# Modulation blocks of two row blocks by 512 columns instead of four by 256, and the sums of both layers as 48 rows of one full PSUM bank

## The chip, the cores and the metric

One core of a Trainium2 chip runs the whole program. The metric is the device time in microseconds of one execution; lower is better. TensorE does the matrix products, VectorE and ACT (ScalarE) the element-wise work, SyncE (SP) issues the weight loads, and ACT and GpSimd issue some small ones. TensorE writes to PSUM, eight banks of 512 fp32 columns a partition.

## The reference

Two blocks in a row, for 256 tokens of width 2048, fp32. The first mixes a gated linear recurrence, an mLSTM and a block attention, projects, adds, and attends to a memory. The second has two layers (a pooling layer, then latent attention with 16 heads), and each layer is steered by modulations, which are what the change is about:

```python
shift, scale, gate = jnp.split(jax.nn.silu(c) @ ada_w[i] + ada_b[i], 3, axis=-1)
h_lat = rms_norm_2(x, pre_norm[i]) * (1 + scale[:, None]) + shift[:, None]
shift_c, scale_c, gate_c = jnp.split(jax.nn.silu(c_ctx) @ ada_w[i] + ada_b[i], 3, axis=-1)
h_ctx = rms_norm_2(ctx, pre_norm[i]) * (1 + scale_c) + shift_c
...
x = x + gate[:, None] * rms_norm_2(y_lat, post_norm[i])
```

`ada_w` is 2 layers x 2048 rows x 6144 columns, 96 MB of the kernel's 307 MB read, and it is multiplied by two vectors only (c for the latents, c_ctx for the context). The columns of a layer are shift (2048), scale (2048) and gate (2048). They aren't needed before the second block: shift and scale of layer 0 before `pu3`, the gate of layer 0 before `po`, layer 1's shift and scale before `cq`, its gate before the last product's results are used.

## The kernel before, in words

**Weight products.** Each product (`Product`, a list in the order of the program: kv, win_a, win_b, win_c, mixo, xq, xo, the pool products pu, pg and pgate, po, then cq, mg01, ckv, kr, mg23, eight pairs of uq and ukv, mo) is cut into column groups of 512 and chunks of 512 rows. SP loads a chunk into `raw` (two slots). ACT rounds it into `w_high` (`act_high`, L289), VectorE puts the rest into `w_low` (`dve_low`, L299), and TensorE does three matmuls for each 128x128 block (L484 to L486, `pe_block`): high by high, high by low, low by high, 256 columns for one sequence or 512 for two, 48 in a full chunk. Results are taken out of PSUM by ACT or VectorE. Each engine follows the list in its own order, written out by hand; between engines there are semaphores only.

**Modulations.** They are computed beside the products. A *unit* is 512 KB of `ada_w`: four blocks of 128 rows by 256 columns, loaded by SP (`sp_unit`, L261, into `ada_raw`, two slots, waiting on `ada_link` until the unit two back is used up). VectorE (`dve_unit`) takes each block times a column of silu(c), one value a partition, and adds it to `ada_acc`, for both vectors: eight passes a unit, TENSOR_SCALAR (L410) for the first of a block's sums and SCALAR_TENSOR_TENSOR (L414) for the others. Each pass waits on `ada_link` for the one two back, which wrote the same half. After four units (2048 rows) `ada_acc` holds partial sums on 128 partitions for 256 columns, a *block* of modulations. TensorE sums over the partitions (`pe_ada`, L432, here called a *slab*): one fp32 matmul for each vector, whose weights are `PICK`, 48 columns of zeros with one column of ones at row r, so that the sums come into row r of a 48-row region of PSUM and nothing is added to the other rows. The next block's first pass on VectorE waits for the slab (`ada_summed`). There are 48 blocks, 24 a layer, and 192 units.

**Where the units stand.** `UNITS` gives each chunk its units: kv four in all, win_a, win_c, the pu chunks and xo one, mixo three in four chunks, pg, pgate and po two, each uq and ukv two, moba four. A chunk on VectorE is: `dve_low`, what the stage adds, then its units. Where a unit is a block's last, TensorE does the slab within that chunk (`pe_chunk`: after the second half's second tile), in moba after the last head, and in the attention pairs (`pe_pairs`) for pair a = 0 to 7 ahead of the product tile uq 1 and the scores.

**Rows.** The first 40 slabs go to bank 4, layer 0 in columns 0 to 255, layer 1 in 256 to 511; row 24 v + m for vector v and block m. Three times ACT copies the 48 rows (`act_rows`, L447, 256 columns) and TensorE turns them (`pe_rows`, L467, two transposes) so that VectorE can add the biases and gains (`dve_mods`, `dve_gates`): turn 0 after slab 16 (end of mixo), turn 1 after 24 (in pgate3: ACT's copy at its chunk 0, the transposes at chunk 1, VectorE at chunk 2), turn 2 after 40 (latents). Slabs 16 and 24 wait until the copy before is done. The last eight go to bank 3, which the ukv products use too; VectorE adds each to `LAST_ROWS` (`dve_last_rows`, L456, L458) and turn 3 takes that (mo).

**The attention pairs.** In each step j TensorE does uq and ukv of pair j and the attention of pair a = j - 1, interleaved. VectorE has per pair four units, the maxima (L2309), the reciprocal and scaling of the probabilities (L2315, L2316; TensorE transposes them in L2179), the output product (L2321), and ahead of the next scores (L2168, L2169) the rope (L2147 to L2150). The third unit stands before the scaling of the fourth quarter's probabilities, the fourth unit before that quarter's output product.

**Small things.** 24 vectors (gains, biases, c) come in as rows of `VROW`, 12 loads on ACT's queue and 12 on GpSimd's, are turned by four transposes (L714) and copied to `vectors` (512 columns). `ident`, `blockmask` and `mlmask` have tiles of their own and are loaded by ACT at the start; `mlmask` is first used in mgates (L1098), `blockmask` in mproj (L1160).

Of the kernel before, what the change touches and what calls it, by code (L numbers as in the profile page):

```python
# [8 lines left out]
ACT = mybir.ActivationFunctionType  # L9
# [3 lines left out]
P = 128  # L13
# [61 lines left out]
def vectors(a):  # L75
# [6 lines left out]
        ("lru_conv_w", m(a["lru_conv_w"][0]), 16), ("lru_conv_b", v(a["lru_conv_b"][0]), 4),  # L82
        ("lru_ba", v(a["lru_ba"][0]), 4), ("lru_bx", v(a["lru_bx"][0]), 4), ("lru_lambda", v(a["lru_lambda"][0]), 4),
        ("ml_conv_w", m(a["ml_conv_w"][0]), 24), ("ml_conv_b", v(a["ml_conv_b"][0]), 6),
        ("ml_g", v(a["ml_norm_g"][0]), 6), ("xa_g", v(a["xa_norm_g"][0]), 16), ("final_g", v(a["final_norm_g"]), 16),
        ("ada_b0", v(a["ada_b_2"][0]), 48), ("ada_b1", v(a["ada_b_2"][1]), 48),
        ("pre0", v(a["pre_norm_2"][0]), 16), ("pre1", v(a["pre_norm_2"][1]), 16),
        ("post0", v(a["post_norm_2"][0]), 16), ("post1", v(a["post_norm_2"][1]), 16),
        ("pool_b", v(a["pool_b_grp_2"].rearrange("l g c -> l (g c)")[0]), 16),
        ("pool_s", v(a["pool_scale_2"][0]), 16),  # L90
        ("q_g", v(a["mla_q_norm_2"][0]), 4), ("kv_g", v(a["mla_kv_norm_2"][0]), 4),
# [32 lines left out]
def build(nc, a, out):  # L124
# [52 lines left out]
    with ctx:  # L177
# [30 lines left out]
        assert at <= 4 * P  # L208
        VROW = BIG[:, 76:78, :].rearrange("p a t -> p (a t)")
# [3 lines left out]
        blockmask = sb("blockmask", [P, P])  # L213
        mlmask = sb("mlmask", [P, P])
# [17 lines left out]
        consts_in, vec_in = [sem(f"consts_in{n}") for n in range(3)], [sem("vec_in_act"), sem("vec_in_pool")]  # L232
# [168 lines left out]
        def dve_unit(dve, u):  # L401
            part, us = u % 4, u % 2
            dve.wait_ge(ada_loaded[us], 16 * (u // 2 + 1))
            if part == 0 and u >= 4:

                dve.wait_ge(ada_summed, u // 4)
            for k in range(KC):
                for v in range(2):
                    if part == 0 and k == 0:
                        ins = nc.vector.tensor_scalar(ACC[:, v], ARAW[:, us, k], SC[:, v, 0:1], None, ALU.mult)  # L410
                    else:

                        dve.wait_ge(ada_link, 8 * u + 2 * k + v - 1)
# [2170 lines left out]
```

## Time and profile before

| | |
|---|---|
| Three runs | 2092.23 us median (2091.14 to 2093.05) |
| The profiled execution, its own time | 2092.57 us |
| its span | 2090.8 us |
| TensorE busy | 1846.7 us, 88% |
| VectorE busy | 1534.3 us, 73%; of it L414 583.6, L410 29.7 |
| ACT busy | 809.6 us, 39% |
| TensorE's mean granted clock | 0.922 of full |
| read from HBM | 307 MB, 148 GB/s |
| slabs (L432, L435) | 43.2 + 8.5 us of TensorE, 192 records for 96 matmuls |

The span goes from the first to the last instruction; 1.8 us lie around it. Busy times of one engine are unions, so overlapping instructions count once, and a mean duration can be longer than the distance from one start to the next. An fp32 matmul shows as two records. L12 is line 12 of the kernel. In the rows below a bracket gives the engine's idle time before the instruction and what ended it, and "x4" is a run of four instructions merged into one row, from the first start to the last end.

### The profile page before, as it was taken

What the parts mean: (1) busy time and instruction counts of PE and PEld (TensorE: products, weight loads), DVE (VectorE), ACT (ScalarE), POOL (GpSimd) and SP (SyncE); (2) the same over time, 40 slices, a digit from 0 to 9 for tenths busy, and PEclk for the clock granted to TensorE, in tenths of its full rate; (3) what the DMA queues carried; (4) which work ended last, traced back from release to release, by engine and by line L of the source; (5) the groups of instructions that cost most, each with busy time, mean ns of one, the idle gap of its engine ahead of it and who ended that gap; (6) DMA issues with size and microseconds to landing.
All of it is one profiled execution on the core that took longest, in us unless ns stands there. A gap on an engine that the chain in (4) does not pass through costs nothing.

```text
span 2090.8 us, 27915 instructions
## 1 busy us (share of the span) xinstructions
PE 1846.7 (88%) x10648; PEld 1567.9 (75%) x10648; DVE 1534.3 (73%) x3022; ACT 809.6 (39%) x1269; POOL 7.2 (0%) x18
## 2 busy tenths in 40 slices
PE   7999914599969987899999998999789989999797
PEld 6899903489939976687877886877687876666497
DVE  5888674598768866788779887977872577777444
ACT  6543334143334443423333222333553454443243
POOL 1000000000000000000000000000000000000000
PEclk9999956589969988899999999999899999999798
DMA  6688600068717633434536553654341553333252
GB/s 209 204 263 261 210 0 1 10 219 264 239 61 262 202 101 102 133 109 149 172 123 202 175 195 125 207 184 141 101 142 56 163 166 121 116 111 105 73 182 96
DMA packets 217954, 311.16 MB, mean 149 GB/s; under 512 B 14760, under 2 KB 121560, under 8 KB 217820
## 3 DMA queue, kind: packets, MB, share of 16 engines
q1 hardware_dynamic: 211328, 305.70, 44.9%
q10 hardware_dynamic: 6044, 3.56, 0.6%
q8 instruction: 84, 1.38, 0.3%
q14 instruction: 50, 0.41, 0.1%
q0 software_dynamic: 448, 0.12, 0.0%
HBM read 307.23 MB, written 2.10 MB: 148 GB/s over the span
## 4 chain that ended last, share of the span: by engine, by line
PE 46%; DVE 12%; ACT 3%; issue 1%; DMA 0%; DVEq 0%; ACTq 0%
PE bank L484 13%; PE bank L485 13%; PE bank L486 13%; DVE ada_acc L414 4%; DVE w_low L299 2%; PE bank L2169 2%; PE bank L2168 2%; PE bank L2188 1%; PE bank L432 1%; ACT w_high L289 1%; DVE big L643 1%; PE bank L2179 1%; DVE big L2011 0%; DVE big L2010 0%; PE bank L1650 0%
## 5 line engine op out<-in xcount | busy, mean ns | idle before, releaser
L484 PE MATMUL bank<-operand,w_high 128*128 128x256 f32 (+1 forms) x2720 | 872.6, 321 | 37.4 <-DVE operand L638 13.7
L485 PE MATMUL bank<-operand,w_high 128*128 128x256 f32 (+1 forms) x2720 | 861.1, 317 | 0.0
L486 PE MATMUL bank<-operand,w_low 128*128 128x256 f32 (+1 forms) x2720 | 860.3, 316 | 0.0
L484 PEld LDWEIGHTS bank<-operand,w_high 128*128 128x128 f32 x2720 | 525.3, 193 | 96.2 <-issue 31.1
L289 ACT ACTIVATE w_high<-raw 128x1024 fp32r<-128x1024 f32 (+4 forms) x416 | 397.0, 981 | 501.1 <-PE bank L486 304.5
L414 DVE SCALAR_TENSOR_TENSOR ada_acc<-ada_raw,silu_c,ada_acc 128x256 f32<-128x256 f32 x1440 | 583.6, 482 | 2.1 <-DMA ada_raw<-in_ada_w 0.6
L299 DVE TENSOR_TENSOR w_low<-raw,w_high 128x1024 fp32r<-128x1024 f32 (+4 forms) x416 | 454.0, 1130 | 176.6 <-ACT w_high L289 175.5
L486 PEld LDWEIGHTS bank<-operand,w_low 128*128 128x128 f32 x2720 | 525.1, 193 | 31.3
L485 PEld LDWEIGHTS bank<-operand,w_high 128*128 128x128 f32 x2720 | 525.6, 193 | 30.4
L484 PE MATMUL bank<-operand_small,w_high 128*128 128x512 f32 (+1 forms) x320 | 124.8, 390 | 11.6 <-DVE big L397 5.4
L485 PE MATMUL bank<-operand_small,w_high 128*128 128x512 f32 (+1 forms) x320 | 120.7, 377 | 0.0
L486 PE MATMUL bank<-operand_small,w_low 128*128 128x512 f32 (+1 forms) x320 | 120.5, 377 | 0.0
L484 PEld LDWEIGHTS bank<-operand_small,w_high 128*128 128x128 f32 x320 | 62.9, 197 | 28.9 <-DVE w_low L299 9.8
L486 PEld LDWEIGHTS bank<-operand_small,w_low 128*128 128x128 f32 x320 | 62.8, 196 | 10.8
L485 PEld LDWEIGHTS bank<-operand_small,w_high 128*128 128x128 f32 x320 | 63.1, 197 | 9.2
L410 DVE TENSOR_SCALAR ada_acc<-ada_raw,silu_c 128x256 f32<-128x256 f32 x96 | 29.7, 351 | 54.6 <-PE bank L432 53.4
L334 ACT ACTIVATE big<-bank 128x256 f32<-128x256 f32 x87 | 33.4, 384 | 93.3 <-PE bank L486 92.8
L2250 ACT ACTIVATE big<-bank,small 128x512 f32<-128x512 f32 x32 | 22.0, 689 | 102.6 <-DVE small L2310 99.3
L344 ACT ACTIVATE big<-bank 128x512 f32<-128x512 f32 x53 | 31.3, 598 | 65.2 <-PE bank L486 65.0
L2309 DVE TENSOR_REDUCE small<-bank 128x1 f32<-128x512 f32 x32 | 22.1, 691 | 44.2 <-PE bank L2169 44.2
L432 PE MATMUL bank<-ada_acc,row_picker 128*48 128x256 f32 x160 | 43.2, 393 | 4.0 <-DVE ada_acc L414 4.0
L628 ACT ACTIVATE operand<-big,modulations 128x256 fp32r<-128x256 f32 x64 | 30.8, 505 | 40.9 <-DVE big L643 40.8
(338 smaller groups left out, 1432.6 us busy)
## 6 DMA issues: line engine op xcount, KB each, us to landing
ada_raw<-in_ada_w SPq DMA_DIRECT2D x192, 512.0 KB, 4.0
raw<-in_w_in SPq DMA_DIRECT2D x96, 512.0 KB, 5.2
raw<-in_pool_w_in SPq DMA_DIRECT2D x64, 512.0 KB, 4.9
raw<-in_mla_w_in SPq DMA_DIRECT2D x48, 512.0 KB, 4.5
raw<-in_w_out SPq DMA_DIRECT2D x32, 512.0 KB, 5.5
raw<-in_pool_w_out SPq DMA_DIRECT2D x32, 512.0 KB, 6.0
raw<-in_mla_w_out SPq DMA_DIRECT2D x32, 512.0 KB, 4.6
raw<-in_xa_wkv SPq DMA_DIRECT2D x16, 512.0 KB, 4.7
```

The source lines that it names most:

```text
L289: ins = nc.scalar.activation(view(HI[:, slot, ks, :], False), view(RAW[:, slot, ks, :], True), ACT.Copy)
L299: ins = nc.vector.tensor_sub(view(LO[:, slot, ks, :], False), view(RAW[:, slot, ks, :], True), view(HI[:, slot, ks, :], False).bitcast(F32))
L334: nc.scalar.activation(dest_ap(p, i, n), PB[p.bank[i, n]][:, 0:T], ACT.Copy).then_inc(act_freed, 1)
L344: nc.scalar.activation(d, src, ACT.Copy).then_inc(act_freed, 1)
L414: ins = nc.vector.scalar_tensor_tensor(ACC[:, v], ARAW[:, us, k], SC[:, v, part * KC + k:part * KC + k + 1], ACC[:, v], ALU.mult, ALU.add)
L432: ins = pe.matmul(PB[4][0:48, 256 * layer:256 * layer + 256], PICK[:, 47 - r:95 - r], ACC[:, v, :], start=m == 0 and v == 0, stop=m in (23 ...
L484: pe.matmul(out_, hi, x[:, 0, :], start=first, stop=False, skip_group_check=True)
L485: pe.matmul(out_, hi, x[:, 1, :], start=False, stop=False, skip_group_check=True)
L486: return pe.matmul(out_, lo, x[:, 0, :], start=False, stop=last, skip_group_check=True)
L628: nc.scalar.activation(n["dst"](k, 0), hf_tile(n, k), ACT.Identity, bias=n["shift"](k)).then_inc(xh_ready, 1)
L2168: pe.matmul(bank[:, :], tile(q_of(a)[h])[:, qt * P:(qt + 1) * P], k_of(a, h), start=True, stop=False)
L2169: la_pe.inc(pe.matmul(bank[:, :], BIG[r, q_of(a)[2], qt * P:(qt + 1) * P], KRT[r, :], start=False, stop=True), "s", a, u)
```

## The change

A block becomes 512 columns wide and a unit two row blocks of 128 instead of four, so that a unit is still 512 KB and there are still 192 of them at the same places, but a block now takes eight units and there are 24 blocks. A unit is four passes of 512 columns. Slabs are half as many, with 512 columns each, at every second place of the old ones; all of them go to row 24 layer + 12 v + m of one region, the whole of bank 4 (the first 20) or bank 3 (the last four, after pairs 1, 3, 5 and 7). The rows are copied with 512 columns and turned by four transposes. Turn 0 comes after slab 8, at the same place; turn 1 after slab 13, and moves from pgate3 to pgate2 (ACT at chunk 2, TensorE at chunk 3) and pgate1 (VectorE at chunk 0); turn 2 after slab 20, at the same place; turn 3 as before. `ada_acc` grows by 512 columns, and to make room `vectors` shrinks to 384 columns (three transposes, the vectors in another order and so split otherwise over the two queues, 12 and 12), and the two masks get places in `big` that are free when they are loaded: `mlmask` in mgates and `blockmask` in mproj, ahead of their three weight loads, both on ACT's queue.

```diff
-        ARAW = sb("ada_raw", [P, 2, KC, 256])
-        ACC = sb("ada_acc", [P, 2, 256])
+        ARAW = sb("ada_raw", [P, 2, 2, GW])
+        ACC = sb("ada_acc", [P, 2, GW])
...
-        PV = sb("vectors", [P, 4 * P])
+        PV = sb("vectors", [P, 3 * P])
...
-        blockmask = sb("blockmask", [P, P])
-        mlmask = sb("mlmask", [P, P])
+        blockmask, mlmask = BIG[:, 46, P:2 * P], BIG[:, 18, 0:P]
...
         def sp_unit(sp, u):
-            part, us = u % 4, u % 2
+            part, us = u % 8, u % 2
             if u >= 2:
-                sp.wait_ge(ada_link, 8 * (u - 1))
-            b = u // 4
-            layer, col = b // 24, (b % 24) * 256
-            src = a["ada_w_2"][layer, part * KC * P:(part + 1) * KC * P, col:col + 256]
+                sp.wait_ge(ada_link, 4 * (u - 1))
+            layer, m = divmod(u // 8, 12)
+            src = a["ada_w_2"][layer, 2 * part * P:2 * (part + 1) * P, GW * m:GW * (m + 1)]
...
         def dve_unit(dve, u):
-            part, us = u % 4, u % 2
+            part, us = u % 8, u % 2
             dve.wait_ge(ada_loaded[us], 16 * (u // 2 + 1))
-            if part == 0 and u >= 4:
-
-                dve.wait_ge(ada_summed, u // 4)
-            for k in range(KC):
+            if part == 0 and u >= 8:
+
+                dve.wait_ge(ada_summed, u // 8)
+            for k in range(2):
                 for v in range(2):
                     if part == 0 and k == 0:
                         ins = nc.vector.tensor_scalar(ACC[:, v], ARAW[:, us, k], SC[:, v, 0:1], None, ALU.mult)
                     else:
 
-                        dve.wait_ge(ada_link, 8 * u + 2 * k + v - 1)
+                        dve.wait_ge(ada_link, 4 * u + 2 * k + v - 1)
                         ins = nc.vector.scalar_tensor_tensor(ACC[:, v], ARAW[:, us, k],
-                                                             SC[:, v, part * KC + k:part * KC + k + 1], ACC[:, v],
+                                                             SC[:, v, 2 * part + k:2 * part + k + 1], ACC[:, v],
                                                              ALU.mult, ALU.add)
...
-            if b in (16, 24):
-                pe.wait_ge(rows_moved, 1 if b == 16 else 2)
-            layer, m = divmod(b, 24)
+            if b in (8, 13):
+                pe.wait_ge(rows_moved, 1 if b == 8 else 2)
+            layer, m = divmod(b, 12)
             for v in range(2):
-                r = 24 * v + m
-                if b < 40:
-                    ins = pe.matmul(PB[4][0:48, 256 * layer:256 * layer + 256], PICK[:, 47 - r:95 - r], ACC[:, v, :],
-                                    start=m == 0 and v == 0, stop=m in (23, 15) and v == 1, skip_group_check=True)
+                r = 24 * layer + 12 * v + m
+                if b < 20:
+                    ins = pe.matmul(PB[4][0:48, :], PICK[:, 47 - r:95 - r], ACC[:, v, :], start=b == 0 and v == 0,
+                                    stop=b == 19 and v == 1, skip_group_check=True)
                 else:
-                    ins = pe.matmul(PB[3][0:48, 0:256], PICK[:, 47 - r:95 - r], ACC[:, v, :], start=v == 0, stop=v == 1)
+                    ins = pe.matmul(PB[3][0:48, :], PICK[:, 47 - r:95 - r], ACC[:, v, :], start=v == 0, stop=v == 1)
...
-            for n in range(2):
-                ins = pe.transpose(PB[TURN_BANK[turn]][:, 48 * n:48 * n + 48],
-                                   (ROWS[turn] if turn < 3 else LAST_ROWS)[:, n * P:(n + 1) * P], ident[0:48, 0:48])
+            for n in range(4):
+                ins = pe.transpose(PB[TURN_BANK[turn]][:, 48 * n:48 * n + 48], ROWS[turn][:, n * P:(n + 1) * P], ident[0:48, 0:48])
...
         def slab_after(p, i, j):
-            done = [u // 4 for u in UNITS[p.name, i, j] if u % 4 == 3]
+            done = [u // 8 for u in UNITS[p.name, i, j] if u % 8 == 7]
...
             act.dma_start(SEL, a["sel"]).then_inc(sel_in, 16)
+            act.dma_start(mlmask, a["mlmask"]).then_inc(mask_in, 16)
...
             for n, w in enumerate(("ml_wq", "ml_wk", "ml_wv")):
+                if n == 0:
+                    act.dma_start(blockmask, a["blockmask"]).then_inc(blocks_in, 16)
                 act.dma_start(MW[:, n], a[w][0].rearrange("(t g) i o -> (g i) t o", g=32)).then_inc(mw_in, 16)
...
-                pe_ada(pe, 13)
+                pe_ada(pe, 6)
...
-                    if p is pgate[3] and j == 0:
-                        act_rows(act, 1, 0, 24)
+                    if p is pgate[2] and j == 2:
+                        act_rows(act, 1, 13)
...
-                    if p is pgate[3] and j == 2:
+                    if p is pgate[1] and j == 0:
                         dve_gates(dve, 0, 1)
...
-                if p is pgate[3]:
-                    ready = lambda e, j: pe_rows(e, 1) if j == 1 else None
+                if p is pgate[2]:
+                    ready = lambda e, j: pe_rows(e, 1) if j == 3 else None
...
-                        if p is ukv and n == 3 and j:
-                            pe.wait_ge(rows_added, j)
+                        if p is ukv and n == 3 and j and j % 2 == 0:
+                            pe.wait_ge(rows_added, j // 2)
...
-                    pe_ada(pe, 40 + a)
+                    if a % 2:
+                        pe_ada(pe, 20 + a // 2)
...
-                    dve_last_rows(dve, a)
+                    if a % 2:
+                        dve_last_rows(dve, a // 2)
```

## Rows read from the trace of the kernel before

**Rows 1.** Busy time by stretches (us, engines' busy us and instructions, TensorE's clock, DMA).
```profile
100.00:250.00 150.00, 150.00 (x1218) 145.71 (x1217) 127.94 (x234) 59.99 (x76) 0.00 (x0) 1.00 0.78 249
900.00:1460.00 560.00, 549.35 (x2381) 438.57 (x2379) 466.55 (x935) 162.32 (x218) 0.00 (x0) 1.00 0.50 165
1700.00:1945.00 245.00, 234.27 (x1170) 164.99 (x1169) 191.27 (x464) 103.49 (x197) 0.00 (x0) 0.99 0.36 119
```

**Rows 2.** Groups of instructions by form: VectorE and TensorE (count, busy us, mean ns).
```profile
L2316 DVE TENSOR_SCALAR big<-big,small 128x512 f32<-128x512 f32 x32 | 15.6, 487 | 1.1
...
L391 DVE TENSOR_TENSOR big<-bank,big 128x256 f32<-128x256 f32 x32 | 12.7, 423 | 15.2 <-PE bank L486 15.1
...
L399 DVE TENSOR_TENSOR big<-big 128x512 f32<-128x512 f32 x16 | 11.1, 692 | 0.6
...
L410 DVE TENSOR_SCALAR ada_acc<-ada_raw,silu_c 128x256 f32<-128x256 f32 x96 | 29.7, 351 | 54.6 <-PE bank L432 53.4 <-issue 0.6
...
L414 DVE SCALAR_TENSOR_TENSOR ada_acc<-ada_raw,silu_c,ada_acc 128x256 f32<-128x256 f32 x1440 | 583.6, 482 | 2.1 <-DMA ada_raw<-in_ada_w 0.6 <-DVE small L2310 0.3
...
L432 PE MATMUL bank<-ada_acc,row_picker 128*48 128x256 f32 x160 | 43.2, 393 | 4.0 <-DVE ada_acc L414 4.0
```

**Rows 3.** Timeline, TensorE, around a slab in win_a (start us, us).
```profile
141.27 0.28 PE L486 MATMUL bank<-operand,w_low 128*128 128x256 f32 x1
141.48 1.06 PE L432 MATMUL bank<-ada_acc,row_picker 128*48 128x256 f32 x4
...
142.70 0.28 PE L485 MATMUL bank<-operand,w_high 128*128 128x256 f32 x1
```

**Rows 4.** Timeline, TensorE, score matmuls of a head pair.
```profile
1765.19 1.02 PE L2168 MATMUL bank<-big 128*128 128x512 f32 x2
1766.15 1.12 PE L2169 MATMUL bank<-big 64*128 64x512 f32 x2
```

**Rows 5.** Waits of TensorE: 40 to 100, 900 to 1260, 1260 to 1460 us (total, times, longest).
```profile
PE bank L484 <- DVE w_low L299: 3.1, 2, 1.9
...
PE bank L432 <- DVE ada_acc L414: 1.3, 2, 1.0
PE bank L484 <- DVE w_low L299: 1.1, 1, 1.1
...
PE bank L432 <- DVE ada_acc L414: 1.8, 1, 1.8
```

**Rows 6.** Timeline, VectorE and TensorE, from one pair's third unit to the next scores.
```profile
1768.29 3.26 DVE L414 SCALAR_TENSOR_TENSOR ada_acc<-ada_raw,silu_c,ada_acc 128x256 f32<-128x256 f32 x8
...
1772.20 0.66 PE L2179 MATMUL bank<-ident,big 128*128 128x128 f32 x4 [0.69 <-DVE big L2316]
...
1776.42 1.06 PE L435 MATMUL bank<-ada_acc,row_picker 128*48 128x256 f32 x4
...
1778.95 1.10 PE L2168 MATMUL bank<-big 128*128 128x512 f32 x2
```

**Rows 7.** Timeline, VectorE and TensorE, pair 0 and the start of pair 7.
```profile
1703.03 6.48 DVE L414 SCALAR_TENSOR_TENSOR ada_acc<-ada_raw,silu_c,ada_acc 128x256 f32<-128x256 f32 x16 [0.55 <-DMA ada_raw<-in_ada_w]
...
1709.56 1.06 PE L435 MATMUL bank<-ada_acc,row_picker 128*48 128x256 f32 x4 [2.75 <-DVE ada_acc L414]
...
1713.12 1.55 PE L2168 MATMUL bank<-big 128*128 128x512 f32 x2
...
1941.91 1.16 PE L2168 MATMUL bank<-big 128*128 128x512 f32 x2 [1.98 <-DVE big L2150]
```

**Rows 8.** Timeline: mgates' ACT issue, moba's end, turn 0, a copy of the rows.
```profile
297.22 0.47 ACTq L1051 DMA_DIRECT2D big<-in_sel  x1
...
626.91 0.36 PE L484 MATMUL bank<-operand,w_high 128*128 128x256 f32 x1 [1.20 <-DVEq L890]
...
744.02 0.32 PE L467 MATMUL bank<-ident,big 48*128 48x48 f32 x2
...
1077.07 0.38 ACT L447 ACTIVATE big<-bank 48x256 f32<-48x256 f32 x1 [7.86 <-PE bank L432]
```

More of the change, by code:

```diff
@@ L231, in build @@
         freed = {"dve": dve_freed, "act": act_freed}
-        consts_in, vec_in = [sem(f"consts_in{n}") for n in range(3)], [sem("vec_in_act"), sem("vec_in_pool")]
+        (ident_in, blocks_in, mask_in), vec_in = [sem(n + "_in") for n in ("ident", "blockmask", "mlmask")], [sem("vec_in_act"), sem("vec_in_pool")]
         tok_in = [[sem(f"tok_in{q}{n}") for n in range(4)] for q in range(3)]
@@ L441, in turned, with act_rows @@
         def turned(turn):
-            return PB[TURN_BANK[turn]][:, 0:96].rearrange("p (n v b) -> p v b n", n=2, v=2)
-        def act_rows(act, turn, layer, slabs):
+            return PB[TURN_BANK[turn]][:, 0:192].rearrange("p (n l v m) -> p l v m n", n=4, l=2, v=2)[:, turn // 2]
+        def act_rows(act, turn, slabs):
             act.wait_ge(ada_summed, slabs)
-            nc.scalar.activation(ROWS[turn], PB[4][0:48, 256 * layer:256 * layer + 256], ACT.Copy).then_inc(rows_moved, 1)
-        LAST_ROWS = BIG[0:48, 74, :]
@@ L451, in dve_last_rows @@
-        def dve_last_rows(dve, a):
-            dve.wait_ge(ada_summed, 41 + a)
-            if a:
-                dve.wait_ge(rows_added, a)
-                nc.vector.tensor_tensor(LAST_ROWS, PB[3][0:48, 0:256], LAST_ROWS, ALU.add).then_inc(rows_added, 1)
+            nc.scalar.activation(ROWS[turn], PB[4][0:48, :], ACT.Copy).then_inc(rows_moved, 1)
+        def dve_last_rows(dve, q):
+            dve.wait_ge(ada_summed, 21 + q)
+            if q:
+                dve.wait_ge(rows_added, q)
+                nc.vector.tensor_tensor(ROWS[3], PB[3][0:48, :], ROWS[3], ALU.add).then_inc(rows_added, 1)
@@ L707, in pe_front @@
         def pe_front(pe):
-            pe.wait_ge(consts_in[0], 16)
+            pe.wait_ge(ident_in, 16)
             for kk in range(8):
@@ L712, in pe_front @@
             pe.wait_ge(vec_in[1], 16 * 12)
-            for b in range(4):
+            for b in range(3):
                 ins = pe.transpose(PB[7][:, b * P:(b + 1) * P], VROW[:, b * P:(b + 1) * P], ident[:, :])
@@ L747, in act_front @@
             s(small[:, 63:64], EPS, ACT.Sqrt).then_inc(root_table, 1)
-            for n in (1, 2):
-                act.dma_start(CONSTS[n][0][:, :], a[CONSTS[n][1]]).then_inc(consts_in[n], 16)
             for kk in range(8):
@@ L1487, in dve_mods @@
             dve.wait_ge(rows_turned, turn + 1)
-            two = lambda ap: ap.rearrange("p (b n) -> p b n", n=2)
+            four_cols = lambda ap: ap.rearrange("p (b n) -> p b n", n=4)
             for w in range(2):
-                v.tensor_tensor(two(MODS[:, 2 + w, :]), turned(turn)[:, w, 0:8, :], two(V[f"ada_b{l}"][:, 0:16]), ALU.add).then_inc(md, 1)
-                v.tensor_tensor(two(MODS[:, w, :]), turned(turn)[:, w, 8:16, :], two(V[f"ada_b{l}"][:, 16:32]), ALU.add).then_inc(md, 1)
+                v.tensor_tensor(four_cols(MODS[:, 2 + w, :]), turned(turn)[:, w, 0:4, :], four_cols(V[f"ada_b{l}"][:, 0:16]), ALU.add).then_inc(md, 1)
+                v.tensor_tensor(four_cols(MODS[:, w, :]), turned(turn)[:, w, 4:8, :], four_cols(V[f"ada_b{l}"][:, 16:32]), ALU.add).then_inc(md, 1)
                 mdc[0] += 2
@@ L1509, in dve_gates @@
             dve.wait_ge(rows_turned, turn + 1)
-            two = lambda ap: ap.rearrange("p (b n) -> p b n", n=2)
+            four_cols = lambda ap: ap.rearrange("p (b n) -> p b n", n=4)
             for w in range(2):
-                v.tensor_tensor(two(MODS[:, 4 + w, :]), turned(turn)[:, w, 16:24, :], two(V[f"ada_b{l}"][:, 32:48]), ALU.add).then_inc(md, 1)
+                v.tensor_tensor(four_cols(MODS[:, 4 + w, :]), turned(turn)[:, w, 8:12, :], four_cols(V[f"ada_b{l}"][:, 32:48]), ALU.add).then_inc(md, 1)
                 mdc[0] += 1
```

40 lines of the change are left out of this document (20 added, 20 removed).

## The prediction

> **What bounds the kernel now.** I read the page first (busy shares, then the 40 slices), and then the table by stretches [rows 1], where its shares come apart. From 100 to 250 us TensorE is busy 150 of 150 us at clock 1.00, from 900 to 1460 us 549 of 560, in the attention heads (1700 to 1945) 234 of 245. These are stretches in which modulation blocks run, and VectorE's 78 to 85% beside it is not their limit: an instruction less on TensorE counts there in full, one less on VectorE only where TensorE stood waiting for it. So the reader is to see two things: what one block costs TensorE within a full stream [rows 3], and the few places where TensorE waits behind VectorE's block sums [rows 5 to 7].
>
> **VectorE's unit.** A unit (512 KB, now eight passes over 128x256) takes 3.26 us from start to end (the first row of [rows 6]), the last pass 0.48 of it (mean of L414 [rows 2]), so the pace is (3.26 - 0.48) / 7 = 0.397 us. For 512 columns no such row exists. TENSOR_TENSOR goes from 423 ns at 256 columns to 692 at 512 [rows 2], 0.269 more. Added to the pace: 0.666, and a unit of four is 2.66 instead of 3.17, **0.51 less**. Bounds: if the new passes don't overlap (0.48 + 0.27 = 0.75), 3.0, 0.17 less; if the added columns cost what TENSOR_SCALAR shows (351 ns at 256, 487 at 512 [rows 2], 0.136), 2.13, 1.04 less. I take the middle one, since TENSOR_TENSOR is the row that reads two tensors as the pass does. A block's first unit begins with two TENSOR_SCALAR, 351 ns less the same overlap of 0.085, 0.266 each: 2 x 0.266 + 6 x 0.397 = 2.91 before, 2 x 0.40 + 2 x 0.666 = 2.13 after. Over the kernel 48 x 2.91 + 144 x 3.17 = 596 us become 24 x 2.13 + 168 x 2.66 = 498. Nearly all of these 98 us lie beside a full TensorE. The wait on the link semaphore reaches two passes back as before and stays under the pace.
>
> By the Trainium skill (VectorE: DVE Perf Modes, "The DRAIN you can't avoid") the next instruction doesn't start until the pipe is empty. The pace would then be the duration, 0.48 and 0.75, and a unit would save 0.85 us instead of 0.51. The trace disagrees: eight passes of 0.48 take 3.26 us.
>
> **TensorE's slab.** pe_ada issues two fp32 matmuls, four records. In the stream [rows 3] L486 before it starts at 141.27 and L485 after it at 142.70: 1.43 us in the place of two steps of 0.12 (150 us / 1218 [rows 1]). A slab costs 1.19. How it grows: a stream record of 512 columns takes 549.35 / 2381 = 0.231 [rows 1], of 256 0.123: 256 columns are 0.108. The slab's records pace at (1.06 - 0.39) / 3 = 0.22 for 256 columns [rows 3, 2], twice that, so 256 more make an fp32 record 0.215 dearer. A slab of 512 columns is 1.19 + 4 x 0.215 = 2.05, but there are half as many: 2 x 1.19 - 2.05 = **0.33 saved for each pair of slabs**, the fixed part of one. The score matmul has 512-column fp32 records: two, and 0.96 us after the first the next two, with another count of weight rows [rows 4], which is 0.43 and, at the change, 0.53. With 0.53 for each record a slab is 2.45, and a pair loses 0.07: the upper bound. I take 0.43, because the picker's rows don't change in a slab.
>
> Where TensorE is full: win_a 6 slabs to 3 (-1.0), win_c 6 to 3 (-1.0), mixo 3 to 1 (-1.5), xo 1 to 1 (+0.9), the pool products 14 to 7 (-2.3), po 8 to 4 (-1.3): **-6.2 us**; with the upper bound +2. The slab at moba's end stays one and gets dearer by 0.9 to 1.7 (half clock), but behind it TensorE stands 1.20 us for VectorE's split of the last operand [rows 8]: 0 to +0.7, I take 0.
>
> **TensorE's waits that end with a unit.** In kv it waits 3.1 us for w_low, 1.9 of it in one piece behind the last two units [rows 5]: two times 0.5, **-1.0**. The slab that leaves kv falls into that same wait and gives nothing. From 900 to 1260 it waits 1.1 for w_low behind two units and 1.3 for sums, from 1260 to 1460 1.8 for sums [rows 5]. Of the three waits for sums two (0.3 and 1.8) belong to slabs that go; the third (1.0) ends after eight shorter units. ACT's copy of the rows, which held it in pgate3 for 7.9 us until a slab was done [rows 8], moves to pgate2, where its slab is done two products before; and the next loads queue behind ACT no later than now. Behind a slab that goes VectorE has only w_low to do, while TensorE still has a quarter of a chunk of 48 records of 0.231. So **-4.2**; -2 if half comes back at the next w_low.
>
> **The attention heads.** TensorE stands 0.69 in a head pair, for the scaled probabilities behind the third unit [rows 6]: 0.5 less. Then two paths meet at the scores, 1778.95: VectorE's (fourth unit, output product, split, rope, just before the scores) and TensorE's (slab at 1776.42, one more tile). VectorE's comes 1.0 earlier with two shorter units. TensorE's comes 0.5 + 1.19 earlier in a pair whose slab is gone, and 0.86 - 0.5 = 0.36 later in one with the doubled slab. The later of both decides: -1.0 for pairs 2, 4, 6, +0.35 for 1, 3, 5, and -1.0 for 7, where TensorE stands 1.98 us for the rope [rows 7] and the longer slab lies in that. Sum **-2.9**. Pair 0: TensorE stands 2.75 us for four units in a row, does slab and tile, and reaches the scores at 1713.12 at a fallen clock (two records in 1.55, not 1.02 [rows 7, 4]). Its slab goes. Of the units the second ended 0.55 before 1703.03, the first at 1699.3, and the third's data came 3.7 after that. Now the first ends 0.78 earlier, 1698.5; third from 1702.2 to 1704.9, fourth's data at 1698.5 + 2.66 + 3.7 = 1704.9, end 1707.6 instead of 1709.5; rope 1.4 more: scores at 1709.0, **-4.1**, or -2.5 if the clock falls all the same and the landing takes longer.
>
> **The rest.** The rows are turned by four transposes instead of two. Two take 0.32 [rows 8], so turns 0 and 1, in a full stretch, cost +0.2 each, turn 2 lies in ACT's copy of them and the norm behind, turn 3 at half clock +0.4: **+0.8**. One transpose less for the vectors: **-0.1**. The copies on ACT and VectorE double their columns beside a busy TensorE. The two masks' issues leave ACT's front, where the table load hides them; the one in mgates falls into ACT's wait for the gate rows, the one in mproj pushes the weight loads by one issue (0.47 [rows 8]) ahead of a table load whose sigmoids wait for VectorE's convolution anyway, and VectorE needs the mask only after six of these. Uncovered they cost 0.47 each. The vectors stay 12 and 12 issues: 0.
>
> Sum: -6.2 - 1.0 - 4.2 - 2.9 - 4.1 + 0.8 - 0.1 = **-17.7 us** against the profiled execution's own 2092.6, 0.3 above the median shown: **2074.5** in terms of that median.
>
> **Rivals.**
> (a) The fixed part isn't saved: a 512-column record paces at 0.53. For it: the score rows between tiles [rows 4]; against: the same rows within a tile. 4 x 0.10 more for some 20 slabs that count: 2082.5.
> (b) The waits come back: VectorE's shorter units only move them to w_low, to ACT or to the landing, which at 3.7 is longer than a unit of 2.66 where units stand in a row. The 12.2 us of waits and heads shrink to about 4: 2083. Against it: with 3.17 a unit the landing was waited for in one place, 0.55 us [rows 7].
> (c) Both, and dearer turns: 2090, no change to be told. Within 0.2% is within 4.2 us, about what a measurement of this kernel can tell.
> (d) Slower, by the slab alone: it blocks the stream in the middle of a chunk. It decides from (17.7 + 4.2) / 24 = 0.91 us above my 2.05, a record pace of 0.66. At full clock nothing comes near (0.53 at most); at half clock it is 0.86. That would need the granted clock to fall at slabs, which it does in none of the full stretches (1.00 [rows 1]). At 0.86 for all 24: 24 x 1.7 = 41 more, 2116.
> (e) More than forecast: units at the TENSOR_SCALAR slope, 1.04 less: kv and heads 4 more, and a fallen clock avoided behind pair 7 as behind pair 0: 2068.
>
> **Chances.** Forecast 0.60, (a) 0.12, (b) 0.12, (c) 0.07, (d) 0.04, (e) 0.05. The forecast's own range is 2070 to 2080, its small terms and which short idle times draw the clock down in the sparse stages. To hold 8 in 10 the range takes in (a) and (b), and (e): 2068 to 2084. Faster by over 0.2%: all but (c) and (d), 0.89; same 0.07; slower 0.04.
>
> **What would show it.** In the profile after: a unit's four passes in about 2.75 us from start to end, VectorE's busy time down by some 95 us; L486 before a slab and L485 behind it 2.3 us apart; no wait of TensorE for ada_acc after 900 us, none for L2316 above 0.3; the heads' periods alternating by about 1.3 us. The prediction is wrong if slabs cost 2.4, if TensorE's waits for w_low grow by what its waits for sums lose, or if head pairs with a slab lose more than the others win.

## The result and the profile after

The changed kernel takes 2064.82 us (median of six, 2063.43 to 2067.62); the kernel before stood at 2092.4 beside it (six executions, 2084.91 to 2093.39). The ratio is 0.9874 (95% interval 0.9859 to 0.9890): 27.6 us faster, where 17.7 was forecast, and 3.2 below the low end of the range. The profiled execution took 2065.26, its span is 2063.5.

The page's busy times, and then VectorE's and TensorE's groups by form (count, busy us, mean ns), the answers to [rows 2]:

```profile
PE 1826.5 (89%) x10559; PEld 1552.1 (75%) x10559; DVE 1437.9 (70%) x2250; ACT 810.0 (39%) x1269; POOL 7.2 (0%) x18
```

```profile
L413 DVE SCALAR_TENSOR_TENSOR ada_acc<-ada_raw,silu_c,ada_acc 128x512 f32<-128x512 f32 x720 | 490.6, 747 | 6.5 <-DMA ada_raw<-in_ada_w 4.3 <-issue 0.6
...
L409 DVE TENSOR_SCALAR ada_acc<-ada_raw,silu_c 128x512 f32<-128x512 f32 x48 | 21.1, 483 | 51.2 <-PE bank L431 50.9
...
L431 PE MATMUL bank<-ada_acc,row_picker 128*48 128x512 f32 x80 | 39.9, 622 | 0.0
...
L434 PE MATMUL bank<-ada_acc,row_picker 128*48 128x512 f32 x16 | 7.7, 602 | 0.0
```

VectorE is busy 96.4 us less (1534.3 to 1437.9; forecast 98). Busy time by stretches, shifted to the same work, the answer to [rows 1]:

```profile
100.00:250.00 150.00, 150.00 (x1213) 145.29 (x1212) 115.75 (x140) 59.63 (x75) 0.00 (x0) 1.00 0.77 251
887.00:1445.00 558.00, 551.29 (x2362) 439.92 (x2360) 429.25 (x612) 165.66 (x222) 0.00 (x0) 0.99 0.51 166
1685.00:1922.50 237.50, 232.21 (x1159) 162.54 (x1157) 175.90 (x338) 103.52 (x197) 0.00 (x0) 1.00 0.39 122
```

TensorE is as full as before and issues the same work in less time. A slab in win_a, the answer to [rows 3]:

```profile
114.80 0.28 PE L482 MATMUL bank<-operand,w_low 128*128 128x256 f32 x1
115.01 1.92 PE L431 MATMUL bank<-ada_acc,row_picker 128*48 128x512 f32 x4
116.86 0.39 PE L480 MATMUL bank<-operand,w_high 128*128 128x256 f32 x1
```

From L482 before the slab to L480 behind it are 2.06 us. The next record follows 0.22 later, as before, and these 2.28 us stand in the place of two steps of 0.12: a slab costs 2.04, and the forecast was 2.05. TensorE's waits (total, times, longest) from 37 to 98 and from 1247 to 1444 us are the answers to [rows 5]; from 892 to 1247 nothing is left to list:

```profile
PE bank L480 <- DVE w_low L298: 4.1, 3, 3.2
...
PE bank L480 <- DVE big L396: 5.4, 1, 5.4
```

The waits for `ada_acc` and w_low behind units are gone from the pool stages, as forecast. In kv the slab that left went into the wait for w_low, whose longest piece grew from 1.9 to 3.2. In the attention heads, the answers to [rows 6, 7] are these. The first row is VectorE in pair 0; then comes TensorE at pair 0's scores, at pair 2's last probabilities and scores, at pair 3's slab, and at the last pair's scores.

```profile
1687.97 5.54 DVE L413 SCALAR_TENSOR_TENSOR ada_acc<-ada_raw,silu_c,ada_acc 128x512 f32<-128x512 f32 x8 [1.19 <-DMA ada_raw<-in_ada_w]
...
1694.89 1.12 PE L2164 MATMUL bank<-big 128*128 128x512 f32 x2 [1.05 <-DVE big L2146]
...
1752.97 0.66 PE L2175 MATMUL bank<-ident,big 128*128 128x128 f32 x4 [0.18 <-DVE big L2313]
...
1759.25 1.13 PE L2164 MATMUL bank<-big 128*128 128x512 f32 x2 [0.56 <-DVE big L2146]
...
1788.75 1.92 PE L434 MATMUL bank<-ada_acc,row_picker 128*48 128x512 f32 x4
...
1919.50 1.13 PE L2164 MATMUL bank<-big 128*128 128x512 f32 x2 [0.61 <-DVE big L2146]
```

Four passes take 2.74 us from start to end (a row of moba below shows it), a pace of (2.74 - 0.75) / 3 = 0.66 as forecast.

**Where the 27 us came from.** For this table the start of each TensorE instruction in one trace is set against that of the same instruction in another; an entry is how much the distance to the trace of before changes over a stretch. "Again" is the second trace of the changed kernel, "narrow" one with narrow passes, both from the experiments below. The row for the pool ends behind po's last slab, at 1457 us.

| stretch of before, us | forecast | after | again | narrow |
|---|---|---|---|---|
| front, to 50 | -0.1 | -2.6 | -2.8 | -1.7 |
| kv, to 106 | -1.0 | +0.4 | +1.6 | +2.5 |
| win_a, to 256 | -1.0 | -1.0 | -1.0 | -1.0 |
| mLSTM, to 431 | 0 | +3.3 | +1.9 | +1.5 |
| win_c, to 572 | -1.0 | -1.0 | -1.0 | -1.0 |
| moba, to 628 | 0 | -3.7 | -3.6 | +0.4 |
| mixo, xq, to 766 | -1.3 | -1.4 | -1.4 | -1.4 |
| cross, xo, to 860 | +0.9 | -1.3 | -0.5 | -0.7 |
| pool, po, to 1457 | -7.6 | -8.1 | -8.7 | -6.2 |
| latents, to 1697 | 0 | +1.0 | +0.6 | +1.1 |
| pair 0, to 1727 | -4.1 | -4.2 | -4.3 | +0.5 |
| pairs 1 to 7, to 1943.5 | -2.9 | -3.8 | -3.8 | +1.7 |
| last pair's scores, to 1962 | 0 | -4.5 | -4.5 | -4.6 |
| the end | +0.4 | -0.4 | -0.5 | -0.2 |
| sum | -17.7 | -27.3 | -28.1 | -9.0 |

### The profile page after: what moved, and what is told of

Same layout as the page of the kernel before. It is cut to its first block and busy times, and to the rows that moved or that the text cites. A ratio compares the mean times of both kernels' runs of the same rounds, so it can differ in the third digit from the quotient of the medians.

```text
span 2063.5 us, 26961 instructions
## 1 busy us (share of the span) xinstructions
PE 1826.5 (89%) x10559; PEld 1552.1 (75%) x10559; DVE 1437.9 (70%) x2250; ACT 810.0 (39%) x1269; POOL 7.2 (0%) x18
## 5 line engine op out<-in xcount | busy, mean ns | idle before, releaser
L480 PE MATMUL bank<-operand,w_high 128*128 128x256 f32 (+1 forms) x2720 | 869.2, 320 | 37.1 <-DVE operand L634 13.3
L482 PE MATMUL bank<-operand,w_low 128*128 128x256 f32 (+1 forms) x2720 | 859.6, 316 | 0.0
L480 PEld LDWEIGHTS bank<-operand,w_high 128*128 128x128 f32 x2720 | 524.5, 193 | 95.4 <-issue 28.2
L482 PEld LDWEIGHTS bank<-operand,w_low 128*128 128x128 f32 x2720 | 524.3, 193 | 31.3
L413 DVE SCALAR_TENSOR_TENSOR ada_acc<-ada_raw,silu_c,ada_acc 128x512 f32<-128x512 f32 x720 | 490.6, 747 | 6.5 <-DMA ada_raw<-in_ada_w 4.3
L480 PE MATMUL bank<-operand_small,w_high 128*128 128x512 f32 (+1 forms) x320 | 125.2, 391 | 11.6 <-DVE big L396 5.4
L482 PE MATMUL bank<-operand_small,w_low 128*128 128x512 f32 (+1 forms) x320 | 121.0, 378 | 0.0
L480 PEld LDWEIGHTS bank<-operand_small,w_high 128*128 128x128 f32 x320 | 63.2, 198 | 30.2 <-DVE w_low L298 9.8
L482 PEld LDWEIGHTS bank<-operand_small,w_low 128*128 128x128 f32 x320 | 63.0, 197 | 10.9
L409 DVE TENSOR_SCALAR ada_acc<-ada_raw,silu_c 128x512 f32<-128x512 f32 x48 | 21.1, 483 | 51.2 <-PE bank L431 50.9
L1730 DVE TENSOR_TENSOR big<-big 128x542 f32<-128x542 f32 (+3 forms) x40 | 28.6, 715 | 25.2 <-ACT big L343 22.4
```

Source lines behind the costliest of these rows:

```text
L413: ins = nc.vector.scalar_tensor_tensor(ACC[:, v], ARAW[:, us, k], SC[:, v, 2 * part + k:2 * part + k + 1], ACC[:, v], ALU.mult, ALU.add)
L480: pe.matmul(out_, hi, x[:, 0, :], start=first, stop=False, skip_group_check=True)
L482: return pe.matmul(out_, lo, x[:, 0, :], start=False, stop=last, skip_group_check=True)
L1730: st.inc(v.tensor_tensor(TA[d % 2][:, :, 0:width], src[:, :, 0:width], src[:, :, 2 ** d:2 ** d + width], ALU.add), f"a{d}", g, n)
```

## The experiments

**Both kernels once more.**

> The kernel before, unchanged, profiled once more. The measured gain was 27.6 us where 17.7 was forecast; in the two traces the terms without a change of TensorE's clock come out as forecast (a pair of slabs 0.33 less, a unit 0.51 less), and the excess sits where the clock fell in one trace and not in the other. Theory A, the clock's falls belong to the kernel: this trace shows them at the same places (half clock in the front's transposes up to 17.5 us, in pair 7 from 1943 to 1957, full clock behind the kv wait at 89.7), and its time is within 1 us of 2092. Theory B, they are a draw of the execution: one or more of these places comes out otherwise, each moves the time by 1 to 5 us, and the time lies anywhere from 2085 to 2094.

> The changed kernel, unchanged, profiled once more. Theory A: pair 7 runs at full clock from 1919 to 1930, kv falls to half clock for 3 us behind its 3.2 us wait at 86.2, the projections at 336 us take 6 us before the clock is back, and the time is within 1 us of 2065. Theory B: one or more of these three places comes out otherwise, and the time lies anywhere from 2063 to 2068.

They took 2090.55 and 2064.50 us. Between the two traces of before the only step above 0.3 us is the front's 2.2: there TensorE's transposes and the products behind them run at half pace (0.21 us a record) until 17.8 us in the one, and the transposes at 0.11 from 13.5 us in the other. The same eight transposes, in before and in before again:

```profile
13.68 1.94 PE L603 MATMUL bank<-ident,big 128*128 128x128 f32 x8 [0.29 <-ACT big L610]
```

```profile
13.44 1.12 PE L603 MATMUL bank<-ident,big 128*128 128x128 f32 x8 [0.69 <-ACT big L610]
```

So 2.2 us of the front can change between two executions of one kernel. All the traces of this document together say a little more. Of the four with the front of before, two are slow there (before and the filled one) and two fast; the ten with the changed front all reach full pace between 12.9 and 15.4 us, and their fronts are 1.6 to 2.8 us shorter than that of the first trace. Whether the change makes the early return likelier isn't shown.

The last pair's scores are the same in both traces of each kernel (half clock from 1943 to 1957 before, full clock until 1932 after), which speaks for theory A there. In kv, the mLSTM and the cross attention the two traces of the changed kernel differ by 1.2, 1.4 and 0.8 us in either sense: theory B, in small.

**Narrow passes, wide slabs.**

```diff
-            for k in range(2):
-                for v in range(2):
...
+            for n in range(8):
+                h, k, v = n // 4, n // 2 % 2, n % 2
+                acc, raw = ACC[:, v, 256 * h:256 * h + 256], ARAW[:, us, k, 256 * h:256 * h + 256]
...
```

> The changed kernel with each of VectorE's passes over 256 columns again: eight to a unit (3.26 us from start to end as before instead of 2.74), slabs and all else as changed. It leaves the merged slabs alone to be paid for. My forecast's terms: the units were to give 1.0 in kv, about 1.3 of the waits for sums, 0.5 for each of seven head pairs and 1.4 of pair 0, some 7 us, so 2072 here and 20 us under before (slabs gone 6, waits that went with their slab, pair 0 and even pairs through the missing slab). Rival 1, the wider passes gave most of the gain (98 us of VectorE's time come out somewhere): 2080 or more. Rival 2, the units' time also decides the clock in pair 7 (the wait before its scores is over 1 us again): 4.5 us on top, 2077.

2086.55 us (2078.76 to 2087.57, seven executions; before beside it 2091.76), ratio 0.9966 (0.9954 to 0.9979). My own expectation of 2072 missed by 14, and rival 1 holds: 21.7 of the 27.6 us are lost when VectorE's passes are narrow again. (The other half of the comparison, wide passes with the narrow slabs of before, was not run.) The profiled execution was the lowest, so it was profiled again.

> The kernel with narrow passes once more, for a profile: of its seven executions the profiled one took 2078.8 us and the six others 2085.0 to 2087.6, so that its trace shows 13.5 us above the changed kernel where the median is 21.7 above. Theory: the other 8 us are TensorE's clock at places where the trace shown happened to keep it (pair 7 at full clock from 1933, and the mLSTM's projections and sums, 340 to 430 us, 4 us shorter than after); a profile of a 2086 us execution shows half clock there and the same durations otherwise. Rival: they are waits behind VectorE that come and go with the landing of the weights; then the clock is the same and TensorE's idle time differs.

2083.58. Its column in the table is 18.3 above the changed kernel, and 17 of these are where VectorE leads: kv's first half 0.9, moba 4.1, the pool stages' waits 1.9, pair 0 4.7, pairs 1 to 7 5.5. The last pair keeps its clock here too, so rival 2 of the run before falls: with the slab of 1.92 us the wait ahead of its scores is 1.13 and not 1.98. Against the first narrow trace this one is 2.5 slower in kv, where the first one kept full clock, and 1.9 slower from 256 to 431, where it had a longer full stretch. The rest up to the median of 2086.55 no trace shows.

**Slabs in pieces.** Each slab matmul as two of 256 columns, back to back. (Each half has a start flag of its own here, and some of the sums come out wrong, presumably by that; the number and the size of the instructions are the intended ones.)

```diff
+                for h in (slice(0, 256), slice(256, 512)):
...
-                    ins = pe.matmul(PB[4][0:48, :], PICK[:, 47 - r:95 - r], ACC[:, v, :], start=b == 0 and v == 0,
+                        ins = pe.matmul(PB[4][0:48, h], PICK[:, 47 - r:95 - r], ACC[:, v, h], start=b == 0 and v == 0,
```

> The changed kernel with each 512-column slab matmul split into two of 256 (eight records to a slab instead of four, back to back), all else as changed. In the trace after, a merged slab costs 2.05 us and an old one 1.19. Theory 1: the 0.33 saved for a pair is the price of breaking into the stream and going back to it (the gaps ahead of the first record and behind the last), not of a matmul: splitting costs nothing, a slab stays at 2.05 to 2.1 and the time at 2065. Rival: it is a price of each matmul, 0.16 a piece: a slab is 2.38, and with 19 slabs where TensorE is full the time is 2071.

```profile
115.75 0.28 PE L484 MATMUL bank<-operand,w_low 128*128 128x256 f32 x1
115.96 1.93 PE L432 MATMUL bank<-ada_acc,row_picker 128*48 128x256 f32 x8
117.82 0.39 PE L482 MATMUL bank<-operand,w_high 128*128 128x256 f32 x1
```

2068.76 us (2066.39 to 2069.82). The profiled execution took 2066.39 and lies 1.1 behind after, 0.8 of it in the front, and no stretch behind 50 us moves by more than 0.2. From L484 before the slab to L482 behind it are 2.07 us where after has 2.06. Theory 1 holds: more matmuls in one visit cost 0.01 us. Then each slab in two visits:

```diff
-                    if slab is not None and h == 1 and n == 1:
-                        pe_ada(pe, slab)
+                    if slab is not None and h == 1 and n in (1, 2):
+                        pe_ada(pe, slab, (n - 1,))
...
+                if att and a % 2:
+                    pe_ada(pe, 20 + a // 2, (1,))
```

> The changed kernel with its slab cut into two visits: the matmul of the first vector where it was, that of the second one product tile later. The columns are the same, the breaks in the stream twice as many. Theory: the fixed price of a visit is 0.33 us (0.09 ahead, 0.04 and 0.09 within, 0.10 behind), so some 22 slabs add 7 us: 2072. Rival: the fixed part hangs on the pair of matmuls, as the wait for ada_acc does: 2065.

```profile
115.54 1.06 PE L431 MATMUL bank<-ada_acc,row_picker 128*48 128x512 f32 x2
116.53 0.38 PE L481 MATMUL bank<-operand,w_high 128*128 128x256 f32 x1
...
117.44 1.06 PE L431 MATMUL bank<-ada_acc,row_picker 128*48 128x512 f32 x2
118.43 0.39 PE L481 MATMUL bank<-operand,w_high 128*128 128x256 f32 x1
```

Each half visit costs 1.18 (the record ahead of it starts at 115.33: 116.53 - 115.33 - 0.12, and 0.10 behind). Two cost 2.36 and one 2.04: the visit's price is 0.3 us, and the trace moves by 0.31 to 0.36 at each slab. The time is 2077.78 (2076.26 to 2079.17), 13 more and not 7: in the trace the last pair's clock falls (half from 1936 to 1950, +3.3) though the wait ahead of its scores is 0.61 as in after. It falls 6 us behind the scores' start (1 us in before), in a wait of 1.75 that after has too, so the wait at the scores isn't all that decides it. And the stretch from moba to xo loses some 3 beside its slabs.

**Where the narrow passes cost.** In the heads alone (the loop above for the last 32 units), and in moba alone (for its four):

> The changed kernel with narrow passes (eight of 256 columns) in the 32 units of the attention heads alone. Theory 1, by the steps of the two traces: pair 0 loses 1.5 to 3, pairs 1 to 7 lose 0.5 (with a slab) or 1.0 (without), 5.5 in all, and pair 7's clock stays or falls (0 or 4.5): 2072 to 2077, so that half and more of what all narrow passes cost lies in the heads. Rival: the heads are worth only the 3.5 of seven thirds units, and the rest of the 21.7 lies in the stages before: 2069.

2074.74 (2071.21 to 2080.28), 9.9 more; in the trace 10.0 from 1697 on: pair 0 4.5, pairs 1 to 7 5.5. The last pair's clock holds.

> The changed kernel with narrow passes (eight of 256 columns) in the four units of moba alone. In the two traces moba is 4.0 us shorter after, although its slab got 1.7 us dearer, and I had put it at 0 to +0.7; both traces with narrow passes everywhere give these 4 us back between 577 and 628 us. Theory: VectorE sets the time of these four heads (busy 9.7 of 10 us from 590 to 610), so each unit counts, 4 times 0.51, and the clock in their gaps adds the rest: 2 to 4 us, 2067 to 2069. Rival: moba's gain is the clock's draw alone; then narrow units there cost nothing: 2065.

2068.97 (2067.32 to 2070.34), 4.2 more; in the trace moba is 4.1 longer. The theory holds. A unit of moba in VectorE's timeline with what stands around it, and the stretch's busy times (PE, PEld, DVE, ACT, POOL), of before and then of after:

```profile
602.88 0.69 DVE L1454 TENSOR_REDUCE small<-big 128x2 f32<-128x512 f32 x1
603.60 0.17 DVE L1455 TENSOR_SCALAR small<-small 128x2 f32<-128x2 f32 x1
603.80 3.26 DVE L414 SCALAR_TENSOR_TENSOR ada_acc<-ada_raw,silu_c,ada_acc 128x256 f32<-128x256 f32 x8
606.98 0.42 DVE L1474 TENSOR_TENSOR big<-bank,big 128x256 f32<-128x256 f32 x1
```

```profile
590.00:613.00 23.00, 14.93 (x41) 9.46 (x41) 22.27 (x53) 7.60 (x21) 0.00 (x0) 0.65 0.34 108
```

```profile
601.96 2.74 DVE L413 SCALAR_TENSOR_TENSOR ada_acc<-ada_raw,silu_c,ada_acc 128x512 f32<-128x512 f32 x4
```

```profile
589.00:612.00 23.00, 14.92 (x43) 9.11 (x43) 22.10 (x43) 7.51 (x21) 0.00 (x0) 0.70 0.39 118
```

Before, VectorE stands nowhere from 589.8 to 616.3 us: unit, output, scaling, next maxima, unit. TensorE's waits for the scaled probabilities from 577 to 628 us, before and after:

```profile
PE bank L1395 <- DVE big L1465: 6.5, 5, 2.1
```

```profile
PE bank L1391 <- DVE big L1461: 5.2, 4, 1.6
```

The units of neighbouring heads start 6.25 us apart before and 5.75 after: a shorter unit counts there in full, although TensorE is busy for only 14.93 of the 23 us.

**Idle time and the clock.** The next runs put idle matmuls (`fill`: identity times 384 columns of the vectors into a bank that nobody reads) into TensorE's waits, first at the end of the last pair:

```diff
+                    if j == 8:
+                        fill(pe, 2)
                     output(a, 0)
```

> The changed kernel with idle matmuls (identity times the vectors, into a bank that nobody reads) ahead of TensorE's waits at the end of the last head pair: two of 384 columns, 1.3 us, ahead of each of its four output products and six, 3.9 us, ahead of the turn of the last rows, where it stands 1.75, 1.94, 1.94 and 4.82 us. Nothing of the computation changes. Theory, idle time makes the clock fall: it stays at full from 1926 to 1953, where it was at half for 15 us, and the time falls by 3 to 5 us: 2061. Rival, the clock falls by something else than TensorE's idle time: the half stretches stay, and the time is the same or 1 us longer, 2065 to 2066.

2066.75 (2064.27 to 2071.99), no gain. The profile shows two opposite parts:

```profile
1926.52 1.16 PE L2188 MATMUL bank<-big 128*128 128x128 f32 x8 [0.45 <-ACT big L2267]
...
1940.44 1.05 PE L2188 MATMUL bank<-big 128*128 128x128 f32 x8
1946.36 7.08 PE L2443 MATMUL bank<-vectors,ident 128*128 128x384 f32 x12 [4.87 <-DVEq L883]
```

Ahead of the outputs the fills kept the clock at full to 1945, and the last output ended 2.7 us earlier, counted from the pair's scores. The six for the turn stood behind the stage's end (a wait for all engines), so they ran only when it was over, on a fallen clock: 7.08 us. With these moved ahead of the stage's end, and fills in kv and the latents:

> The changed kernel with idle matmuls of 384 columns (0.65 us each at full clock) on TensorE in waits that the trace after shows: four ahead of kv's last chunk (3.2 us of waiting there), four and five around the turn of rows 2 (3.6 and 4.1), eight ahead of the first cq chunk (7.1), two ahead of each of the last pair's output products (1.8 to 1.9), and six at the end of the heads, now ahead of the stage's end and not behind it, where they did 7 us of harm in the run before this one. Theory, TensorE's own idle time makes its clock fall, and the stretches behind such a wait then run at half: kv gives 1.2, the latents 3 to 6, the last pair 2.7 (measured in the run before this one), the start of the last product 0.5: 2056 to 2059, with full clock where it was half at 86 to 89, 1455 to 1461, 1472 to 1478 and 1932 to 1953. Rival: the fills meet a clock that has fallen already, take twice their time and push the work behind them: 2064 or more.

```profile
1919.51 1.16 PE L2194 MATMUL bank<-big 128*128 128x128 f32 x8 [0.45 <-ACT big L2274]
...
1934.33 4.04 PE L469 MATMUL bank<-vectors,ident 128*128 128x384 f32 x12
1939.31 0.42 PE L464 MATMUL bank<-ident,big 48*128 48x48 f32 x4 [0.95 <-DVEq L889]
```

2053.97 us (2053.60 to 2054.18), ratio to before 0.9823 (0.9808 to 0.9838), 10.9 below the changed kernel: the best version here. TensorE's busy us (the idle matmuls are in them) and clock behind those waits, first after, then with fills (the same work, shifted):

```profile
86.00:89.00 3.00, 2.79 (x13) 0.50 0.57 173
1446.00:1461.00 15.00, 7.28 (x19) 0.55 0.23 70
1465.00:1478.00 13.00, 5.93 (x28) 0.62 0.25 81
1931.00:1953.00 22.00, 13.20 (x56) 0.69 0.16 49
```

```profile
84.00:87.00 3.00, 2.35 (x9) 1.00 0.64 191
1440.00:1455.00 15.00, 13.64 (x43) 0.89 0.21 70
1458.00:1471.00 13.00, 10.69 (x48) 0.88 0.26 82
1924.00:1943.00 19.00, 16.75 (x90) 1.00 0.17 51
```

Not all of the 10.9 us is the fills' own. Between the profiled executions the gain is 11.5, and 5.2 of it lie in the mLSTM (2.8), the cross attention (1.6) and the pool (0.8), where no fill stands (4.4 against the second trace of after). Where they stand, kv gains 1.3, the latents 1.0 and everything from the last pair's scores on 4.2. And kv kept its clock without a fill in the first narrow trace and in the one with moba alone, so its 1.3 can be a draw too.

The same question put to the kernel before, in the wait of 1.98 us [rows 7] ahead of the last pair's scores (two fills behind the slab):

> The kernel before with two idle matmuls of 384 columns behind the last head pair's slab, 1.3 of the 1.98 us in which TensorE stands for the rope of pair 7. In both traces of before the clock falls right behind that wait, from 1943 to 1957, and in both of after, where the wait is 0.61, it does not. Theory: that wait is what makes it fall, so the 4.5 us between 1942 and 1960, which my forecast left to a rival of 0.05, are a consequence of the shorter units: 2088 here. Rival: the fall belongs to the sparse work behind the scores or to where the execution happens to stand, and only moves: 2092.

Here are TensorE's stretches without the fills (before), then the place with them, and the first stretch again with them:

```profile
1943.00:1957.00 14.00, 12.52 (x24) 0.52 0.00 1
1957.00:1981.00 24.00, 14.57 (x65) 0.72 0.16 44
```

```profile
1935.47 1.56 PE L2219 MATMUL bank<-vectors,ident 128*128 128x384 f32 x4
1937.52 1.13 PE L2168 MATMUL bank<-big 128*128 128x512 f32 x2 [0.49 <-DVE big L2150]
```

```profile
1939.00:1953.00 14.00, 9.80 (x31) 0.83 0.01 2
```

2088.56 (2084.65 to 2090.46) beside 2092.35, ratio 0.9984 (0.9976 to 0.9993): 3.8 less, as the theory had it: the wait ahead of the scores is 0.49 there, and the clock of the stretch 0.83 and not 0.52. Last, all fills in the kernel before:

> The kernel before with the same idle matmuls that took the changed kernel from 2064.8 to 2054.0 us, and two more ahead of the scores of pair 7. It asks what the change is worth where TensorE's clock in the last pair and behind those waits is at full in both. Theory: the forecast's 17.7 plus the 3.7 to 4.2 of moba, some 22, so 2054 + 22 = 2076, and the 5 us by which the measured gain of 27.6 exceeds that were the clock of pair 7. (In kv the four idle matmuls, 2.6 us, are longer than the 1.9 of waiting there: +0.7 of its own.) Rival: the clock is not part of the difference; then the distance stays at 27 to 28 and the time is 2081 to 2082.

```profile
1943.00:1957.00 14.00, 12.38 (x46) 1.00 0.00 1
```

2084.12 (2083.08 to 2084.39; before beside it 2093.64). The distance to the filled changed kernel is 30.1 us (28.9 if each is taken against the kernel before that ran beside it) and not 22: the theory fails as a sum. Stretch by stretch, from 1943.5 on the two filled kernels now gain the same (0.1 apart, where after was 4.9 ahead of before), so the last pair's clock did leave the difference. But where there are no fills the clock differs against this kernel: front 2.4, 256 to 431 2.5, cross and xo 1.0. Without these three the traces are 23.6 us apart.

## Why the prediction was wrong

**Right.** The bound, and what each edit changes: a unit at a pace of 0.66, the slab at 2.04 and 0.33 saved a pair (win_a, win_c and mixo to 0.1), the waits for sums gone, the slab of kv lost in its wait, pair 0 at -4.2 for -4.1 with the scores 0.3 us from the place given. Rivals (a) to (d) are refuted: records pace at 0.43, and nothing took the place of the waits in the pool stages. VectorE did wait longer for `ada_raw` (4.3 us in sum against 0.6).

**Wrong: "an instruction less on TensorE counts there in full, one less on VectorE only where TensorE stood waiting for it".** The rule is right, but I applied it to three full stretches and to waits that end with a unit, and took "The slab at moba's end" as all of moba. There the wait ends with L1465, a scaling that stands behind a unit in VectorE's queue. Up to the slab moba came out 4.6 us shorter, 2.0 of it four shorter units at 0.51 and the rest a clock that came back earlier; the slab itself and the wait behind it cost 0.9 more, a little over the +0.7 that I had as its bound. That is -3.7, and narrow passes in moba alone cost 4.1. The view that would have shown it is the busy time of a sparse stretch: VectorE 22.27 of 23 us.

**Wrong: "a fallen clock avoided behind pair 7 as behind pair 0", put in rival (e) at 0.05.** Its place and mechanism came true: -4.5 us or more in every trace of the changed kernel and its variants but the one with two visits, and 3.8 by the fill in before. That the one with two visits lost it with the same wait of 0.61 leaves open what else sets the moment. The wait fell from 1.98 to 0.61 because VectorE came 0.5 sooner and the slab took 0.86 longer, both terms of my own sum. A wait that is nearly gone ahead of a stretch at half clock deserved the main line, 2070.

**Off in size.** Pairs 1 to 7 gave 3.8 for 2.9: pair 1 gained 0.1 and pair 3 lost 0.1 where each was to lose 0.35. Before, TensorE had waited 0.16 for the rope at pair 1's scores and 0.97 instead of 0.69 for pair 3's probabilities, which I had not counted. The pool stages gave 8.1 to 8.7 for 7.6. The latents lost 0.6 to 1.0 for 0. What makes that up I did not separate, except that the last rows' copy became 0.59 for 0.38 us and its four transposes ran at half clock; in xo the slab's +0.9 is there, but the clock of the stretch outweighs it.

**Not the change's, or not shown to be.** Of the front's 2.6 the second trace of before has 2.2. In kv the clock fell in the 3.2 us wait and gave back 1.2 to 2.5. In the mLSTM (+3.3, +1.9) and around the cross attention the clock returns at another moment in each kernel; one kernel's executions agree within a few us all the same. What sets these moments stays open, and with it some 3 us of the 27.6 either way. In the first pair of traces these four stretches miss their forecasts by -2.5 (front), +1.4 (kv), +3.3 (mLSTM) and -2.2 (cross), and that they cancel is luck. So of the 9.6 us that these traces gained beyond the forecast, moba and the last pair's scores make 8.2.

The expectation of 2072 for narrow passes had its own mistake: it paid the units 0.5 a pair and 1.4 in pair 0, but the even pairs' 1.0 and all of pair 0's 4.1 hang on VectorE being early as well as on the slab being gone. Narrow passes with the slab gone took back all of pair 0's gain (+0.5 against before); that the slab put back would do the same is argued and not run. Where two paths meet, a gain that needs two edits can't be shared out between them.

## What to carry to other kernels

A full stretch says what bounds it; a sparse one doesn't, so read for each sparse stretch which engine never stands in it, and cost what stands ahead of the instruction waited for, whatever it belongs to. Work that breaks into a matmul stream pays by the visit (0.3 us here), so make visits few and wide. Where TensorE waits in a dependent stretch (here 1.8 to 7 us at a time), price the work behind the wait at either clock, and try idle matmuls in it, on the near side of any wait for all engines.

## What the runs showed of the hardware

- A visit of fp32 matmuls in a stream of rounded ones costs 0.3 us beside its columns, with one, two or four matmuls in it: 0.09 ahead, 0.13 within, 0.10 behind. A record takes 0.216 us at 256 columns and 0.429 at 512.
- Fills of 1.3 us in waits of 1.75 to 1.94 us, and 4.0 us of them ahead of the stage's end, held the granted clock at 1.00 (2.4 GHz) where it had been 0.69 (1931 to 1953), over half of it at 0.5 (1.2 GHz).
- Eight passes of VectorE over 128x256, 0.48 us each, start 0.40 apart, and four over 128x512, 0.75 each, 0.66 apart.
- Up to 17.8 us the views of before show a granted clock of 1.00 while transposes pace at the half rate of 0.21 us. The trace's first record of the clock stands at 17.8 us in before and at 12.2 in before again, and at both places the pace doubles; ahead of that record the 1.00 rests on nothing, and the durations have to be read. By the Trainium skill (TensorE: Matmul & The Clock Gate, Part 1) how many matmuls run cold at a kernel's start varies from run to run. The two traces of before agree: their full pace begins 5.6 us apart, and 2.2 us of their time lie there.
